# The first layer's mixer of a two-layer decoder step, from four program blocks to one

## What is computed

```python
z = h @ w_in                                   # 1024 -> 3080: value, gate, q/k/v, out gate, 8 scalars
glu = z[..., :512] * sigmoid(z[..., 512:1024])
ca, new_buf_a = causal_dwconv(glu, buf_a, conv_a_w)        # 31 taps, 512 channels
ya = silu(layernorm(ca + conv_a_b))
qkv, new_buf_qkv = causal_dwconv(z[..., 1024:2560], buf_qkv, conv_qkv_w)   # 4 taps, 1536 channels
q, k, v = split(silu(qkv)); q, k = l2norm(q) * 128**-0.5, l2norm(k)        # 4 heads of 128
beta = sigmoid(z4); g = -exp(a_log) * softplus(z4b + dt_bias)
od, s_new = gated_delta(q, k, v, g, beta, s0)  # chunks of 64 rows: a triangular inverse per chunk, then a scan
od = rmsnorm(od) * silu(gate)
y = concat([ya, od]) @ w_out
```

## Time and profile before

| what | us |
|---|---|
| median of 3 runs (2534.22 to 2537.0) | 2535.35 |
| the profiled execution, its own time | 2538.01 |
| its span in the profile | 2536.2 |
| PE busy / DVE busy / ACT busy | 2054.6 / 1281.5 / 778.8 |
| column block, 24 x 3.88 | 21.0 to 117.5 |
| convolution block | 117.5 to 236.5 |
| delta block | 236.5 to 437.8 |
| first gather of layer 0's tail | 501.9 |

### The profile page before, as it was taken

The page is one execution under the profiler, slowest core; times in us unless marked ns, Lnnn a source line. Parts: engine busy times, 40 slices in busy tenths (PEclk is TensorE's granted clock), DMA queues, the critical chain, the costliest instruction groups (busy, mean ns, idle before and its releaser), DMA issues. The chain is left out here.

```text
span 2536.2 us, 25647 instructions
## 1 busy us (share of the span) xinstructions
PE 2054.6 (81%) x9026; PEld 1021.2 (40%) x9026; DVE 1281.5 (51%) x3157; ACT 778.8 (31%) x2275; POOL 639.3 (25%) x645
## 2 busy tenths in 40 slices
PE   7894884698887798786699999976987887988766
PEld 5683773353222243222244464553532222432222
DVE  0085753355667757675410030023556677576754
ACT  1142000033444434444311131121334444344443
POOL 0000000024444444433101100000244444444341
PEclk9986775899999999997899999998899999999978
DMA  7894993489999999999759856843899999999995
GB/s 243 304 344 156 330 336 104 181 345 426 427 427 427 427 427 414 427 427 427 296 229 379 331 202 264 324 185 137 344 427 427 427 427 427 426 425 427 427 427 244
DMA packets 129652, 874.98 MB, mean 345 GB/s; under 512 B 16100, under 2 KB 29924, under 8 KB 45419
## 3 DMA queue, kind: packets, MB, share of 16 engines
q0 software_dynamic: 92160, 662.74, 63.0%
q1 hardware_dynamic: 37363, 210.60, 23.1%
HBM read 861.98 MB, written 118.81 MB: 387 GB/s over the span
## 5 line engine op out<-in xcount | busy, mean ns | idle before, releaser
L1433 PE MATMUL tail_acc<-tail_ring,tail_diag 128*128 128x512 f32 x1216 | 593.4, 616 | 116.9 <-ACT tail_diag L1292 115.6
L1180 DVE CUSTOM_DVE_ANT_0 tail_ring<-tail_ring,all_h 128x1024 f32<-128x1024 f32 x344 | 418.7, 1223 | 236.9 <-DMA tail_ring<-in_peer_uv,tail_idx 236.4
L1433 PE MATMUL tail_acc<-mid_wring,tail_diag 128*128 128x512 f32 x832 | 413.8, 625 | 99.4 <-ACT tail_diag L1292 99.2
L1573 POOL DMA_INDIRECT tail_ring<-in_peer_uv,tail_idx x344 | 365.9, 1064 | 483.2 <-PE tail_acc L1433 411.8
L1573 POOL DMA_INDIRECT mid_wring<-in_peer_uv,tail_idx x232 | 236.8, 1020 | 981.3 <-DVE all_x L1065 501.5
L1433 PEld LDWEIGHTS tail_acc<-tail_ring,tail_diag 128*128 128x128 f32 x1216 | 213.8, 191 | 481.2 <-ACT tail_diag L1292 307.9
L1180 DVE CUSTOM_DVE_ANT_0 mid_wring<-mid_wring,all_h 128x1024 f32<-128x1024 f32 x232 | 283.2, 1223 | 175.1 <-DMA mid_wring<-in_peer_uv,tail_idx 173.6
L1286 ACT ACTIVATE tail_gelus<-tail_dots 128x1 f32<-128x1 f32 x576 | 116.2, 202 | 727.2 <-DVE tail_dots L1180 726.9
L1433 PEld LDWEIGHTS tail_acc<-mid_wring,tail_diag 128*128 128x128 f32 x832 | 147.9, 193 | 354.1 <-ACT tail_diag L1292 224.4
L1687 PE MATMUL mix_acc<-mid_wring,all_hT 128*128 128x512 f32 x576 | 276.8, 616 | 1.5 <-PEq L80 1.4
L1292 ACT ACTIVATE tail_diag<-all_ident,tail_weights 128x128 f32<-128x128 f32 x512 | 205.5, 401 | 22.8 <-PE tail_acc L1433 5.8
(11 more groups left out here) (363 smaller groups left out, 2081.5 us busy)
## 6 DMA issues: line engine op xcount, KB each, us to landing
mid_wring<-in_w_qkv SPq DMA_DIRECT2D x18, 2048.0 KB, 8.4
out_kv_s<-in_cache_kv_w SPq DMA_DIRECT2D x8, 4064.0 KB, 49.1
mix_ring<-in_kT POOLq DMA_DIRECT2D x16, 1024.0 KB, 7.7
mix_ring<-in_v_rows POOLq DMA_DIRECT2D x16, 1024.0 KB, 11.6
ab_ring_w<-in_w_in_ab SPq DMA_DIRECT2D x6, 2048.0 KB, 10.8
mix_ring<-in_kT POOLq DMA_DIRECT2D x16, 768.0 KB, 9.1
mix_ring<-in_v_rows POOLq DMA_DIRECT2D x16, 768.0 KB, 10.5
mid_wring<-in_w_out SPq DMA_DIRECT2D x4, 2048.0 KB, 10.4
```

Of the source, the lines that this page charges most:

```text
L1180: V.tensor_tensor_reduce(out=u, in0=u, in1=h[:, g, :], scale=1.0, scalar=0.0, op0=ALU.mult, op1=ALU.add, accum_out=dots[:, n:n + 1]).then_ ...
L1433: last = mm(acc[g][:, c * 512:(c + 1) * 512], diag[:, n % DIAGS, :], v[:, c * 512:(c + 1) * 512], start=first, stop=final)
L1573: pool.indirect_dma_start(slot(r), None, table, bass.IndirectOffsetOnAxis(ap=idx[:, j, i:i + 1], axis=0)).then_inc(landed[r], 16)
```

## The change

The blocks for columns, convolution and delta become one, `conv_delta_phase`. TensorE multiplies the 12 blocks of q, k and v first, with two accumulators instead of six, and VectorE runs their 4-tap convolution as they come. The sums of squares for the norms of q and k are collected into 8 rows with a sliding one-column window, so one root and one reciprocal of 8 rows replace two of 128 x 1152, and the result is spread again by eight matmuls (`widen`). Then the three tile lanes start together with a fourth lane, `branch`: 12 more column blocks in halves (`job_key`), glu, and all 124 taps of the 31-tap convolution on VectorE (`tap_key`, four taps to one unit of the key). `main` joins them from key 40 on; the layer norm stands between its steps. The input weights, histories and the state are laid out on the host. The weights now use the ring `wring`, and `w_out` is loaded in the mixer. The cache copies are cut into 48 pieces of at most 2.1 MB and stand in SyncE's program where `roll` says. The norm of the delta output, after the scan, also collects its sums in 8 rows and spreads them again.

```diff
-    PE_A = 1
-
-    diag_groups = [(True, c, k, min(4, CAW - k)) for c in range(4 - PE_A, 4) for k in range(0, CAW, 4)]
-    n_a = len(diag_groups)
-    diag_groups += [(False, c, 0, CQW) for c in range(12)]
...
-                conv_taps(CAW, 4 - PE_A, pa, sa, wa, ca, lambda c: wa[:, c, 31:32])
-                dve.wait_ge(group_done, n_a)
-                for c in range(PE_A):
-                    ch.step(V.tensor_scalar(ca[:, 4 - PE_A + c, :], p_hist[:, c * 512:c * 512 + NTOK],
-                                            wa[:, 4 - PE_A + c, 31:32], None, ALU.add))
...
+def conv_delta_phase(nc, K, T, wring, w_in, w_out_in, mixT, rolls):
...
+    EXPS, MAIN = at[0, "exps act"], 40
+    job_key = lambda j, half: 5.5 + 1.15 * (2 * j + half)
+    JOBS_A = [(kind, c) for c in range(4) for kind in ("gate", "value")] + [("out", c) for c in range(4)]
+    MEAN_KEY = MAIN + 9.5
...
+                roll(4)
+                sp.wait_ge(col_ready, 4)
+                sp.dma_start(wring[:, 0], T["w_ab"][:, 2]).then_inc(w_in[0], 16)
+                sp.dma_start(S0[:].rearrange("p b h n -> p (b h n)"), T["state_rows"]).then_inc(state_in, 16)
+                roll(3)
+                sp.wait_ge(col_ready, 8)
+                sp.dma_start(wring[:, 1], T["w_ab"][:, 3]).then_inc(w_in[1], 16)
+                roll(2)
+                sp.wait_ge(col_ready, 12)
+                sp.dma_start(wring[:, 0], T["w_ab"][:, 4]).then_inc(w_in[0], 16)
+                roll(3)
+                sp.dma_start(T["out_conv_a_s"][0, :, 0:26, :], T["state_conv_a"][0, :, 4:30, :]).then_inc(stored, 16)
+                sp.wait_ge(a_ready, 7)
+                sp.dma_start(wring[:, 1], T["w_ab"][:, 5]).then_inc(w_in[1], 16)
+                sp.wait_ge(tail_q_out, 3)
+                sp.dma_start(T["out_conv_qkv_p"][0, 0], tail_q[0:3, :]).then_inc(stored, 16)
+                sp.dma_start(T["out_conv_qkv_s"][0], tail_q[3:27, :]).then_inc(stored, 16)
+                roll(10)
+                sp.wait_ge(a_ready, 12)
+                for c in range(2):
+                    sp.dma_start(wring[:, c], T["w_out0"][:, c]).then_inc(w_out_in[c], 16)
+                sp.wait_ge(tail_a_out, 1)
+                sp.dma_start(T["out_conv_a_p"][0, 0], tail_a[0:30, :]).then_inc(stored, 16)
+                sp.dma_start(T["out_conv_a_s"][0, :, 26:30, :], tail_a[30:62, :]).then_inc(stored, 16)
+                roll(len(late))
+                sp.wait_ge(turn["main"], at["main", "c3 S dve"] + 1)
+                sp.dma_start(T["out_delta_p"][0, 0].rearrange("h k v -> k h v"), S[:]).then_inc(stored, 16)
+                sp.wait_ge(turn[2], len(order[2]))
+                for b in range(DEC_B):
+                    sp.dma_start(T["out_delta_s"][0, b].rearrange("h k v -> k h v"), S0[:, b, :, :]
+                                 ).then_inc(stored, 16)
+                sp.wait_ge(stored, 16 * (6 + DEC_B))
...
+                def column(i):
+                    s = i // 4
+                    if i % 4 == 0:
+                        pe.wait_ge(w_in[s % 2], 16 * (s // 2 + 1))
+                    if i >= 2:
+                        pe.wait_ge(z_ready, i - 1)
+                    for k in range(KC):
+                        last = mm(acc_of(i), wring[:, s % 2, k, i % 4 * 128:i % 4 * 128 + 128], hT[:, k, :],
+                                  start=(k == 0), stop=(k == KC - 1))
+                    last.then_inc(col_ready, 1)
+
+                def sums(i):
+                    m = QC[i]
+                    if i == 0:
+                        pe.wait_ge(delta_in, 16 * 5)
+                        for t in range(3):
+                            pe.wait_ge(turn[t], EXPS + 1)
+                    pe.wait_ge(square_done, i + 1)
+                    mm(bank[0][0:8, 0:NTOK], win[:, 7 - m:15 - m], sqs[:, i % 2, :], start=(i == 0), stop=(i == 7)
+                       ).then_inc(sum_step, 1)
...
+                    pe.wait_ge(rs_ready, 1)
+                    if i >= 2:
+                        pe.wait_ge(norm_done, i - 1)
+                    mm(bank[1 + i % 2][:, 0:NTOK], over(ident[0:8, m], 1, 128), rs[:], start=True, stop=True
+                       ).then_inc(wide_ready, 1)
...
+                    yield at[t, "cross pe"]
+                    begin(pe, t, "cross pe")
+                    pe.wait_ge(norm_done, 8)
+                    pe.wait_ge(tail_q_out, 3)
...
+                    for j, (kind, c) in enumerate(JOBS_A):
+                        s = {"gate": 3, "value": 4, "out": 5}[kind]
+                        for half in range(2):
+                            yield job_key(j, half)
+                            if half == 0:
+                                pe.wait_ge(w_in[s % 2], 16 * (s // 2 + 1))
+                                if j == 0:
+                                    pe.wait_ge(z_ready, 11)
+                                elif j == 1:
+                                    pe.wait_ge(z_ready, 12)
+                                elif j == 8 or kind == "gate":
+                                    pe.wait_ge(sig_done, j // 2)
+                                elif j == 9 or kind == "value":
+                                    pe.wait_ge(glu_done, (j - 1) // 2)
+                                else:
+                                    pe.wait_ge(gate_done, j - 9)
+                            for k in range(4 * half, 4 * half + 4):
+                                last = mm(acc_of(j), wring[:, s % 2, k, c * 128:c * 128 + 128], hT[:, k, :],
+                                          start=(k == 0), stop=(k == KC - 1))
+                        last.then_inc(a_ready, 1)
+                    yield job_key(12, 0)
+                    pe.wait_ge(last_a_ready, 2)
+                    pe.wait_ge(gate_done, 3)
+                    for c in range(4):
+                        last = nc.tensor.transpose(bank[6][0:62, c * 128:c * 128 + 128], last_a[:, c, :], ident[:])
+                    last.then_inc(tail_a_ready, 1)
...
+                lanes = Lanes([tile(0), tile(1), tile(2), branch(), main()])
+                for i in range(4):
+                    column(i)
+                pe.wait_ge(delta_in, 16 * 5)
+                lanes.run(at[0, "wide pe"])
+                column(4)
+                lanes.run(at[0, "cross pe"])
+                for i in range(5, 8):
+                    column(i)
+                    if i > 5:
+                        sums(2 * i - 12)
+                        sums(2 * i - 11)
+                for i in range(8, 12):
+                    column(i)
+                    sums(i - 4)
+                q_tails(0)
+                q_tails(1)
+                for i in range(8):
+                    widen(i)
+                q_tails(2)
+                lanes.run()
...
+                for i in range(4, 8):
+                    take(4 + i)
+                    silu(i)
+                act.wait_ge(eps_done, 1)
+                A(rs[:], rs[:], ACT.Sqrt).then_inc(root_done, 1)
+                copy_tail(0)
+                copy_tail(1)
+                for i in range(8, 12):
+                    silu(i)
...
+                    taps = [(c, k) for c in range(4) for k in range(CAW)]
+                    begun = job_key(1, 1) + 0.3
+                    tap_key = lambda i: max(job_key(2 * taps[i][0] + 1, 1) + 0.3, begun + i * 0.25)
...
+                            ch.settle(lag=1)
+                            ch.step(STT(out=ca[:, c, 0:SEQ], in0=pa[:, c, k:k + SEQ], scalar=wa[:, c, k:k + 1],
+                                        in1=ca[:, c, 0:SEQ], op0=ALU.mult, op1=ALU.add))
+                            ch.settle(lag=1)
+                            ch.step(STT(out=dst, in0=smp, scalar=wa[:, c, k:k + 1], in1=dst, op0=ALU.mult,
+                                        op1=ALU.add))
...
+                    c = 0
+                    for i in range(len(taps)):
+                        while c < 4 and tap_key(i) > job_key(2 * c + 1, 1) + 0.2:
+                            yield job_key(2 * c + 1, 1) + 0.2
+                            glu(c)
+                            c += 1
+                        yield tap_key(i)
+                        tap(i)
...
-            G, delta_loaded, delta_loads = delta_inputs(P0, T)
-            zT, conv = P0.sb("zT", [128, 24, NTOK]), P0.sb("conv", [128, 12, NTOK])
-            with ExitStack() as c3:
-                W = WeightRing(Phase(nc, c3, "ab_ring"), T["w_in_ab"][0], IN_AB - 8, 3)
-                first_norm_phase(nc, K, T, hT, W.start)
-                def copies(sp):
-                    roll_cache(sp, T, 0, cache_out)
-                    roll_cache(sp, T, 1, cache_out, range(2))
-
-                columns_phase(nc, "ab", hT, T["w_in_ab"][0], IN_AB - 8, zT, ahead=W, before=delta_loads, after=copies)
-            conv_phase(nc, "cv", K, T, zT, mixT, conv, cache_out)
-            delta_phase(nc, "gd", K, T, G, delta_loaded, hT, zT, conv, mixT, cache_out)
-
```

(44 more changed lines are left out.)

773 lines of the change are left out of this document (364 added, 409 removed).

## The result

Over 18 runs each, the changed kernel takes 2541.93 us (2536.23 to 2548.49) and the kernel before 2536.11 (2534.22 to 2539.55); the ratio is 1.0021, 95% interval 1.0014 to 1.0029, so some 5 us slower. The forecast was 2527 with the range 2509 to 2551: the time lies inside, the sign is wrong. One profiled execution of the changed kernel took 2536.72 (span 2534.9), near its fastest, and 1.3 less than the profiled execution of the kernel before. So the profile shows the mechanism, and the medians the size.

A forecast was written before the change was run, and what follows sets the result against it. SyncE's in-order queue of cache copies was taken to bound layer 0's mixer; 2 us from the mixer and 6.6 from the tail made -8.6 against 2535.35, so 2527 us, range 2509 to 2551.

The forecast's parts named there:

- What bounds the block: Layer 0's mixer: SyncE's queue of copies and the stores behind it end the block, at 436 against 437.79 before.
- The engines would be done at 343: Layer 0's mixer: TensorE and VectorE finish about 343, 95 us before they do now, but the mixer gives only 2 us.
- The idle queue ahead of the wait: SyncE's queue before `a_ready` 7: idle for 58 us, with the DMA share near 0 from 126 to 185.
- the idle engines behind 340: End of layer 0's mixer: TensorE and VectorE stand still from about 343 to 436.
- Rival C: End of layer 0's mixer: stores land beside the copies, the queue doesn't hold the block; 2435, or 2437 with landing; chance 0.08.
- so `a_ready` reaches 7 at 184.5: SyncE's wait for the seventh gate column: ends at 184.5, 76 us after the lanes' start; moves the time one for one.
- rival A: Lanes: VectorE's non-overlapping taps (+9) or TensorE's clock fall delay `a_ready` 7 and all copies by 28; 2555; chance 0.20.
- The front: Gates and 12 columns reach 96, then 12 us of root, reciprocal and normalising; lanes start heavy steps at 108.5.
- The lanes: Three tile lanes plus branch: VectorE slightly leads at 13.8 us a level, 3.45 a key unit; 76 us to the seventh product.
- The queue's own length: SyncE's queue from 184.5: copies at 337 GB/s to 426.8, delta stores to 434.8, tail starts at 436.
- The tail: Layer 0's tail finds `w_out` loaded: 35.3 us to the first turn instead of 41.9, gain 6.6, bounds none to 10.4.
- Rival B: Layer 0's tail gives nothing back because another small load lands as late; only 2 us gained, 2533.5; chance 0.14.

## Why the prediction failed on the sign, step by step

**What bounds the block: right.** The end was forecast as the queue's, and the experiments that took copies from behind both waits, left the last ones out or moved the first wait all moved the end. The engines would be done at 343, I wrote; they are at 337.7. The idle queue ahead of the wait, the idle engines behind 340 and the 35 us of the tail are all in the profile after. Rival C (the stores land beside the copies, 2435) has fallen twice, on SyncE's queue and on ScalarE's. On "Queues, rings and completion order" of the Trainium skill's page "DMA: Bandwidth & Descriptors": that completion is not in order for an issuing engine did not help the stores here; what the same section says of turns between queues, taken packet by packet, agrees with the counts of 756 against 757 packets, and with 111.20 against 36.40 us.

**The failed step: "so `a_ready` reaches 7 at 184.5".** It was 195.9 and 195.3. I had written that the end moves with it one for one, and the whole gain was 8.6 us, so an error of 11.4 in one estimate turned the sign. The prediction had allowed 12 us for it in its range, but hardly in its chances: within the forecast one in twenty for slower, and the rest of its 0.23 all for rival A. The error is a sum of several:

```profile
98.65 0.65 PE L427 MATMUL mix_banks<-mix_squares,mix_window 128*8 128x288 f32 x2 [1.57 <-ACT mix_squares L647]
...
104.40 7.58 PE L435 MATMUL mix_banks<-mix_roots,all_ident 8*128 8x288 f32 x16 [4.11 <-DVE mix_roots L968]
...
113.73 0.77 PE L466 MATMUL mix_banks<-mix_conv 128*128 128x128 f32 x2 [0.77 <-ACT all_h L659]
...
131.32 1.05 PE L480 MATMUL mix_banks<-mix_decayT,mix_g_wide 128*128 128x128 f32 x8
...
153.07 2.31 PE L480 MATMUL mix_banks<-mix_decayT,mix_g_wide 128*128 128x128 f32 x24
...
166.57 1.16 PE L480 MATMUL mix_banks<-mix_decayT,mix_g_wide 128*128 128x128 f32 x8 [0.46 <-DVE mix_decayT L804]
...
172.12 5.83 PE L546 MATMUL mix_banks<-all_hT,mid_wring 128*128 128x288 f32 x16
...
181.36 8.64 PE L503 MATMUL mix_banks<-mix_Rk,mix_S_sample 128*128 128x4 f32 x64
189.85 6.02 PE L546 MATMUL mix_banks<-all_hT,mid_wring 128*128 128x288 f32 x16
195.71 1.95 PE L480 MATMUL mix_banks<-mix_decayT,mix_g_wide 128*128 128x128 f32 x16
```

These rows are TensorE's, in the changed kernel. The front: the last sum of squares ends at 99.3, not 96 (among other things columns 8 to 11 come every 6.30 us, not 5.9), and from there to the lanes it takes 14.4, not 12, since the eight spreading products run one by one with VectorE for 7.58. Lanes at 113.73 and not at 108.5: 5.2. The lanes: 82.2 us to the seventh product and not 76. A term is missing, the row at 181.36: the sample tile's 64 matmuls have key 19 and stand ahead of both halves of the product, whose keys are 19.3 and 20.45. I had booked all of the sample tile's long steps behind the seventh product. These 8.64 us are more than the 6.2 that the lanes are late, and the sum was off in two more places that partly cancel. First, it takes 14.5 units of the key for the levels, but the first step `P` has key 9, so that no more than 11.45 stand ahead of 20.45; with its own 3.45 a unit the product would have been due at 174. Second, a level is longer than 13.8: the first matmuls of step `P` (L480) are 21.8, 13.5 and 29.1 us apart. In the first of these stretches VectorE is busy for 21.43 of 21.75 us, so there it does lead, in part with steps that I had booked ahead of the levels; in the last one TensorE is busy for 28.50 of 29.14. That 76 came within 6 us of 82 is luck.

**The clock's share.** The granted clock is 1.00 from 150 to 172 us, but 0.72 from 172 to 178 and 0.69 from 190 to 196, stretches at the full clock and at the lower level in turn: the products at 172.12 and 189.85 take 5.83 and 6.02 us, and 4.15 where the clock is full, 3.6 us lost together. And it differs from execution to execution. Up to the wait, the kernel with the stores on ScalarE's queue is the changed kernel; in its profile the clock is 0.50 from 172 to 178 and from 190 to 196, and the same three rows read

```profile
172.32 7.12 PE L540 MATMUL mix_banks<-all_hT,mid_wring 128*128 128x288 f32 x16
...
182.84 11.51 PE L497 MATMUL mix_banks<-mix_Rk,mix_S_sample 128*128 128x4 f32 x64
...
194.22 6.41 PE L540 MATMUL mix_banks<-all_hT,mid_wring 128*128 128x288 f32 x16
```

They take 4.6 us more, and the seventh product comes at 200.7. In five profiles of kernels with the same code up to the wait it lies between 195.3 and 200.7, and with it the end of the block, as long as the queue ends it.

**The queue's own length: 2.6 us short.** From the end of the wait to the tail's first matmul I had 251.5 us. Five profiles with the same transfers behind the wait, of the changed kernel twice, without taps, of the wait one later and of the closer keys, show 251.8, 254.4, 251.9, 255.5 and 256.6, 254.1 in the mean. The copies ran at 334, 329, 333, 329 and 321 GB/s in them from 350 to 430: the slower the copies, the longer the stretch. The mean adds up to 195.6 + 254.1 = 449.7, against 437.8 some 12 later, less 6.8 in the tail, 5 slower; the medians give 5.8. That it comes so near is in part luck, because the stretches vary by as much from profile to profile: the seventh product by 5 us, the copies behind it by 5, and all that follows the tail's start by 8 (2087.4 to 2095.3 in ten profiles with the same code there). These three are large enough for the 12 us over which the changed kernel's runs spread; how they share in its median is not shown.

**The tail: right.** 35.1 us in place of 41.9, a gain of 6.8; forecast 6.6. Rival B falls.

**Rival A** named the right place (a late `a_ready` 7 and the queue behind it). It was to decide from a delay of 14 us on, the gains of 8.6 and 5 more that can't be told; 11.4 us, with a queue 2.6 us longer, were enough. Of its two causes one was not at work: the taps are 0.56 us apart, as before. The other was there in small: no fall of the clock through all the levels, which was to cost 28 to 37 us, but falls in parts that cost 3.6 us in one profile and 4.6 more in another. The main causes, the front and the order of the keys, it did not name.

## What to carry to other kernels

Where one queue carries bulk copies that depend on nothing and small transfers that wait for engines, every wait on it delays all the bulk behind it: spread the copies so that enough bulk stands ahead of each wait to last until it ends, and no more than is left to do behind the last. Add up each gap; one gap filled alone gave 3.6 us, not clear of the noise, both filled gave 74. When a forecast gain is smaller than the error of an estimate on which the end hangs one for one, the sign is open, and the chances should say so; each step in an order that is set by keys has to be placed by its key before it is booked to a stretch.

## What the runs showed of the hardware

- A separate hardware queue is not a fast lane beside DRAM to DRAM copies of long rows: eight stores of 256 KB took 111.20 us to issue on ScalarE's otherwise empty queue, 36.40 us once the copies went in runs of 4 KB. Beside copies on another queue the packets went one for one, 756 and 757 in 100 us, whatever their sizes. So a load in very small packets holds up all that stands behind it on its queue: SyncE stood 81.45 us in the issue of a weight chunk behind 480 KB in packets under 512 B, with copies on GpSimd's queue.
- Copies from DRAM to DRAM ran at 330 to 339 GB/s beside fully loaded lanes and at 321 to 336 with all engines idle: the compute did not slow them, nor did they slow the compute (the seventh product came at 196.3 to 200.4 in three profiles with copies beside it, at 195.3 to 200.7 in five without).
- The same code with the same work before it was granted a clock of 0.72 in one execution and of 0.50 in another, over the same 6 us; three groups of matmuls behind it took 20.5 and 25.0 us.
- Long and short runs (64 KB and 4 KB) were copied at the same rate, 333 to 335 and 336 GB/s.
